# Four modulation pieces back on VectorE, an earlier first expert choice, and a choice's index work over both halves at once

## The reference, cut to what matters

```python
for i in range(4):                                   # mixers: GLA, SGU, FOX attention, GLA
    mod = silu(c) @ w_mod[i] + b_mod[i]              # 1024 -> 3072: shift, scale, gate
    h = rms_norm(x, norm_pre_g[i]) * (1 + scale) + shift
    x = x + gate * rms_norm(mixer_i(h), norm_post_g[i])
x = x + hybrid_mixer(rms_norm(x))                    # conv, three dilated attentions
u = rms_norm(x)
q = (u @ w_query).reshape(T, 8, 2, 128)              # 8 heads, two half queries
top_s, top_i = top_k(q . sub_keys, 16)               # 16 of 128 in each half
best_s, pos = top_k(top_s[0][:, None] + top_s[1][None, :], 16)      # 16 of 256 pairs
idx = top_i[0][pos // 16] * 128 + top_i[1][pos % 16]
x = x + sum(softmax(best_s) * gelu(u . down[idx]) * up[idx])        # 128 rows a token
```

## Time and profile before

| | |
|---|---|
| median of 3 runs | 1745.24 us (1738.43 to 1745.35) |
| the profiled execution: own time, span | 1739.41 us, 1737.6 us |
| PE, PEld, DVE, ACT, POOL busy | 80%, 41%, 60%, 25%, 28% of the span |
| mean granted clock of TensorE | 0.909 of full |
| moved by DMA | 591.53 MB, 340 GB/s over the span |
| rows of experts gathered by GpSimd | 312.56 MB with the pieces, 45.4% of 16 engines |
| chain that ended last | DVE 8%, DMA 8%, issue 3%, PE 1% |

### The profile page before, as it was taken

One profiled execution on the slowest core, in us unless ns is written; L12 is line 12 of the kernel. 1 busy time (PEld: TensorE's weight loads), 2 busy tenths in 40 slices (PEclk: granted clock), 3 DMA queues, 4 the chain that ended last, 5 costly groups with the idle time before them and its releaser, 6 DMA issues. The chain is left out here.

```text
span 1737.6 us, 13867 instructions
## 1 busy us (share of the span) xinstructions
PE 1393.7 (80%) x4158; PEld 717.6 (41%) x4158; DVE 1047.5 (60%) x2197; ACT 433.1 (25%) x974; POOL 490.7 (28%) x498
## 2 busy tenths in 40 slices
PE   6998988978999999999777777699787647666665
PEld 6454435444444455444354343455333312222222
DVE  3645554553233222313797998788866778877876
ACT  1221413423423421102133232132002221111111
POOL 2101210210000000000445546355344545444441
PEclk9998998989999999999897888798888878898898
DMA  9978884978556776887999989999999999999995
GB/s 386 377 256 303 312 340 171 347 282 295 213 207 219 277 265 242 290 293 265 402 361 357 413 339 403 412 400 413 410 414 414 348 412 422 421 422 421 422 421 248
DMA packets 108941, 591.53 MB, mean 340 GB/s; under 512 B 12450, under 2 KB 12706, under 8 KB 60612
## 3 DMA queue, kind: packets, MB, share of 16 engines
q0 software_dynamic: 67776, 312.56, 45.4%
q1 hardware_dynamic: 41092, 278.10, 42.2%
HBM read 589.55 MB, written 1.05 MB: 340 GB/s over the span
## 5 line engine op out<-in xcount | busy, mean ns | idle before, releaser
L948 PE MATMUL bank<-ring,hT 128*128 128x512 f32 x1888 | 866.6, 615 | 39.6 <-DVE room L1920 12.1
L948 PEld LDWEIGHTS bank<-ring,hT 128*128 128x128 f32 x1888 | 366.5, 198 | 482.2 <-issue 449.8
L877 POOL DMA_INDIRECT room<-in_peer_down,idx x92 | 102.5, 1114 | 525.1 <-DVE idx L1781 401.8
L1798 DVE CUSTOM_DVE_ANT_0 room<-room 128x1024 f32<-128x1024 f32 x180 | 218.6, 1221 | 50.6 <-DMA room<-in_pair,idx 38.4
L1203 PE MATMUL bank<-room 128*128 128x512 f32 x284 | 150.9, 676 | 96.5 <-ACT room L1493 94.2
L1813 DVE SCALAR_TENSOR_TENSOR x<-room,pcoef,x 128x1024 f32<-128x1024 f32 x121 | 155.7, 1287 | 28.0 <-DMA room<-in_peer_up,idx 27.5
L877 POOL DMA_INDIRECT room<-in_peer_up,idx x104 | 114.0, 1096 | 88.6 <-DVE pa L1798 42.3
L1203 PEld LDWEIGHTS bank<-room 128*128 128x128 f32 x284 | 57.5, 215 | 190.8 <-issue 97.2
L849 POOL DMA_DIRECT2D room<-in_w_mod x80 | 42.2, 528 | 326.3 <-DVE room L1567 206.5
L877 POOL DMA_INDIRECT room<-in_pair,idx x88 | 97.0, 1102 | 108.5 <-PE bank L1203 50.6
L927 PE MATMUL bank<-cst,room 128*128 128x128 f32 x424 | 64.7, 297 | 55.3 <-ACT room L1439 24.1
(11 more groups left out here) (304 smaller groups left out, 1527.4 us busy)
## 6 DMA issues: line engine op xcount, KB each, us to landing
ring<-in_wpk SPq DMA_DIRECT2D x248, 1024.0 KB, 7.0
room<-in_w_mod POOLq DMA_DIRECT2D x80, 512.0 KB, 8.2
room<-in_w_mod SPq DMA_DIRECT2D x8, 1024.0 KB, 15.8
room<-in_norm_post_g POOLq DMA_DIRECT2D x4, 512.0 KB, 5.0
rowb<-in_gate_bias SPq DMA_DIRECT2D x4, 512.0 KB, 9.0
room<-in_peer_up,idx POOLq DMA_INDIRECT x104, 12.5
room<-in_peer_down,idx POOLq DMA_INDIRECT x92, 12.4
room<-in_pair,idx POOLq DMA_INDIRECT x88, 14.3
```

Of the source, the lines that this page charges most:

```text
L877: return pool.indirect_dma_start(out=dst, out_offset=None, in_=A[table][0] if table != "pair" else A[table], in_offset=bass.IndirectOffset ...
L948: last = mm(bank[p][:, :], lhs, ring[:, h % 4, k * N:(k + 1) * N], start=(kk == 0), stop=(h == halves[-1] and k == 3))
L1798: v.tensor_tensor_reduce(out=row, in0=row, in1=u_(g // MINE), scale=1.0, scalar=0.0, op0=ALU.mult, op1=ALU.add, accum_out=pa[:, g // TOPK ...
```

## The change

It makes four kinds of edit.

1. Pieces 9, 11, 13 and 15 are summed on VectorE again; TensorE keeps 5 and 7.
2. A chunk's "mod" steps stand behind its "ev", the mixer's steps, "mod_cols" and "mod_gate", and ahead of what is pending; their numbers a block come from a table. One gap moves from behind layer 2's last output block to behind its fourth input block.
3. For tile 0, the first head's scores come one query block earlier, and so does its choice; the ticks stay where they are. In a choice three casts are left out, and the comparison, the product and the reduction work on both halves in one instruction each.
4. The last eight picks are added two a tick from tick 272 on, their last group of four is split in two, and picks 252 and 253 go to TensorE, 254 to VectorE.

```diff
 def out_chunks(t, L):
-            "gap twice"]
+            "gap" if L == 2 else "gap twice"]
...
             b(3, [], [("unit", t, 1), ("forget_sum", t)]),
+            "gap",
             b(4, [], [("quad_T", t, 0), ("quad_S", t, 0)]),
...
-            b(0, name="query", pre=[("norm_in", t, 5)]),
-            b(1, [("score_T", t, 0)], name="query"),
-            b(2, [("score_S", t, 0), ("score_T", t, 1)], name="query"),
+            b(0, [] if t else [("score_T", t, 0)], name="query", pre=[("norm_in", t, 5)]),
+            b(1, [("score_T", t, 0)] if t else [("score_S", t, 0)], name="query"),
+            b(2, ([("score_S", t, 0)] if t else []) + [("score_T", t, 1)], name="query"),
...
-TICKS = PICKS + REST + LEAD[1]
+TICKS = PICKS + REST + 2
-PE_PIECES = (5, 7, 9, 11, 13, 15)
+PE_PIECES = (5, 7)
...
 def on_vector(u):
-    return u < 7 * TOPK or u % 4 == 3 or (u % 2 and (u < MINE or u >= PICKS - 8))
+    return u < 7 * TOPK or (u % 4 == 3 and u < PICKS - 4) or (u % 2 and u < MINE) \
+        or u >= PICKS - 2 or (u % 2 and PICKS - 8 <= u < PICKS - 4)
...
 def added_at(v):
+    if v >= PICKS - 8:
+        return tick_of(PICKS - 2) + (v - PICKS + 8) // 2
     return tick_of(v) + LEAD[v // MINE]
...
-def pieces_at(mm):
-    if mm is None:
-        return 0
-    if mm[2] == "in0":
-        return (4, 4, 3, 2, 2, 2)[mm[3]]
-    return 4 + mm[3] if mm[2] == "out0" else 3
+PIECES_AT = {"in0": (4, 4, 4, 3, 3, 2), "out0": (4, 2), "in1": (4, 4, 4, 4, 3, 3), "out1": (3, 3),
+             "in2": (3, 3, 3, 3, 2, 2, 2, 2), "out2": (4, 2)}
...
         if mm:
             order.append(mm)
-        for _ in range(pieces_at(mm)):
-            if piece < len(PIECES):
-                order.append(("mod", piece))
-                piece += 1
         if mm and mm[2] in ("out0", "out1", "out2") and mm[3] == 1:
             order.append(("mod_cols", int(mm[2][3]) + 1))
...
+            for _ in range(PIECES_AT[name][n] if name in PIECES_AT else 0):
+                order.append(("mod", piece))
+                piece += 1
             order += pending
             pending = []
-            if name == "query" and n == 2:
+            if name == "query" and n == 1:
                 order.append(("choose", 0))
-                rows.tick()
-            if name == "query" and n == 3:
-                rows.tick()
-                rows.tick()
+            if name == "query" and n >= 2:
+                for _ in range(n - 1):
+                    rows.tick()
...
-                    v.tensor_copy(pixf[:, :, :], pix[:, :, :])
...
-                    link(v.tensor_copy(pabf[:, :, :], pab[:, :, :]))
                 elif part == 2:
-                    for c in range(2):
-                        last = v.tensor_tensor(hot[:, c, :, :], const("iota").unsqueeze(1).to_broadcast([P, TOPK, TOPK]),
-                                               pabf[:, c, :].unsqueeze(2).to_broadcast([P, TOPK, TOPK]), ALU.is_equal)
-                    link(last)
...
+                    both = [P, 2, TOPK, TOPK]
+                    link(v.tensor_tensor(hot, const("iota").unsqueeze(1).unsqueeze(1).to_broadcast(both),
+                                         pab[:, :, :].unsqueeze(3).to_broadcast(both), ALU.is_equal))
+                    link(v.tensor_tensor(hot, hot, pix[:, :, :].unsqueeze(2).to_broadcast(both), ALU.mult))
...
+                    link(v.tensor_reduce(psel[:, :, :], hot, X, ALU.add))
...
-                    v.tensor_copy(idx[:, w, :], pidf[:, :]).then_inc(S("picked"), 1)
+                    v.scalar_tensor_tensor(out=idx[:, w, :], in0=psel[:, 0, :], scalar=float(NK), in1=psel[:, 1, :],
+                                           op0=ALU.mult, op1=ALU.add).then_inc(S("picked"), 1)
```

More of the change, by code:

```diff
@@ L272 @@
 DVE_NTH = {u: i for i, u in enumerate(ON_DVE)}
-ADDS = {added_at(v): [v] for v in range(PICKS)}
+ADDS = {k: [v for v in range(PICKS) if added_at(v) == k] for k in range(TICKS)}
 def adds_of(k):
-    return ADDS.get(k, [])
+    return ADDS[k]
 def sums_at(hh):
@@ L289 @@
 EXP_AT = {sums_at(hh): hh for hh in range(T * PH) if hh != PH - 1}
-GROUPS = [(hh * TOPK, TOPK) for hh in range(PH)] + [(MINE + 4 * m, 4) for m in range(MINE // 4)]
+GROUPS = [(hh * TOPK, TOPK) for hh in range(PH)] + [(MINE + 4 * m, 4) for m in range(MINE // 4 - 1)] \
+    + [(PICKS - 4, 2), (PICKS - 2, 2)]
 GROUP_AT = {tick_of(g + n - 1) + 1: i for i, (g, n) in enumerate(GROUPS)}
 def group_of(v):
-    return v // TOPK if v < MINE else PH + (v - MINE) // 4
+    return next(i for i, (g, n) in enumerate(GROUPS) if g <= v < g + n)
 WAY = {"norm_in": 110, "low": 10, "decay": 12, "qk_T": 15, "level": 25, "cross": 30, "heads": 80, "gated_T": 50,
@@ L558, in build @@
         pix = sb("pix", [P, 2, TOPK], U32)
-        pixf = sb("pixf", [P, 2, TOPK])
         ppos = sb("ppos", [P, TOPK], U32)
         pab = sb("pab", [P, 2, TOPK], U32)
-        pabf = sb("pabf", [P, 2, TOPK])
         psel = sb("psel", [P, 2, TOPK])
-        pidf = sb("pidf", [P, TOPK])
         idx = sb("idx", [P, 4, TOPK], U32)
@@ L683, in build @@
         pk2, cand, cand2 = at(AA + 6144, 2 * P), at(AA + 6400, TOPK, TOPK), at(AA + 6656, TOPK * TOPK)
-        hot = at(AA + 6912, 2, TOPK, TOPK)
+        hot = at(AA + 6912, 2 * TOPK * TOPK).rearrange("p (c a b) -> p c a b", c=2, a=TOPK)
         diag = at(DIA, 4, P)
@@ L992, in _ @@
             pe.wait_ge(S("cond"), 1)
-            for piece in PE_PIECES[:2]:
+            for piece in PE_PIECES:
                 piece_columns(piece, use("mod_cols", 0)[1])
@@ L1002, in _ @@
                         pe.wait_ge(S(f"ev{p}"), n // 2)
-                    if L == 0:
-                        for piece in PE_PIECES[2:]:
-                            piece_columns(piece, p)
                     pe.wait_ge(S(f"sums_init{L % 2}"), sums_set(L))
@@ L1759, in choose @@
                     link(v.tensor_single_scalar(pab[:, 1, :], ppos[:, :], 15, ALU.bitwise_and))
-                    link(v.tensor_copy(pabf[:, :, :], pab[:, :, :]))
                 elif part == 2:
-                    for c in range(2):
-                        last = v.tensor_tensor(hot[:, c, :, :], const("iota").unsqueeze(1).to_broadcast([P, TOPK, TOPK]),
-                                               pabf[:, c, :].unsqueeze(2).to_broadcast([P, TOPK, TOPK]), ALU.is_equal)
-                    link(last)
[L1766 to L1769, removed]
-                else:
[L1771 to L1775, removed]
+                    both = [P, 2, TOPK, TOPK]
+                    link(v.tensor_tensor(hot, const("iota").unsqueeze(1).unsqueeze(1).to_broadcast(both),
+                                         pab[:, :, :].unsqueeze(3).to_broadcast(both), ALU.is_equal))
+                    link(v.tensor_tensor(hot, hot, pix[:, :, :].unsqueeze(2).to_broadcast(both), ALU.mult))
+                else:
+                    link(v.tensor_reduce(psel[:, :, :], hot, X, ALU.add))
                     if 4 <= hh < PH + 4:
```

## The result

The changed kernel takes 1756.44 us (median of 10 runs, 1751.95 to 1764.76), the kernel before 1744.86 (10 runs, 1738.43 to 1752.99): 1.0071 times as long, with a 95% interval of 1.0055 to 1.0087. It is slower, by 11.6 us at the medians. I had put 1741 as likeliest and 0.20 on slower by over 0.5%; the time is inside the range of 1720 to 1757 by half a us. Some 5 us of these are the scatter of single executions, as the profiled one of before was 5.5 us under its kernel's median and that of after is at its own. Two executions among all runs here, one of the kernel before and one of the version with the choice's instructions alone, took 2124 us at a granted clock of 0.64 and are in no ratio.

A forecast was written before the change was run, and what follows sets the result against it. TensorE's chain bounds the kernel until about 830 us, then mostly DMA. Terms 1.5 + 5.9 - 24 + 11.3 - 0.9 + 3.5 + 5 + 1.6 = 3.9 us less, predicting 1741 against the median; range 1720 to 1757.

The forecast's parts named there:

- Start and border to layer 1: Start: first block 9.0 us sooner, 1.5 kept (0 to 5). Layer 0 to 1: shorter piece wait, 5.9 gained (4 to 6).
- by 80 us: Sign against the prediction: TensorE's first levels come by 80 us; it expected the first level product at 83 to 85.
- Layer 1: SGU layer: twelve pieces ahead of the gate, 61 to 63 held up in GpSimd's queue; 24 us lost (15 to 28).
- Layer 2 and its output: Moved gap fills TensorE waits, 6.8; shorter piece wait, 2.8; layer 3's "mod_cols", 1.7; 11.3 us gained (6 to 15).
- nothing is lost: Layer 3's start: one block, 7 us, instead of two still covers the norm's about 6 us on VectorE and ScalarE.
- The first choice and the gathers: Transposes cost 0.9 us; six rows fetched sooner gain 3.5 (1.5 to 4); slots freed earlier gain 5 (0 to 9).
- three signs of being wrong: Pieces 61 to 63 landing within 3 us of issue; first levels by 80 us; DMA share 880 to 1060 us unchanged.
- The end: After the last dot product: fewer adds on TensorE, VectorE's last at +4.4 instead of +6.0; 1.6 us gained (1 to 2.5).
- The faster one: Rival, chance 0.34: pieces 61 to 63 land soon, SGU loss 12, start gives 4.5; near 1726 us (1716 to 1732).
- The slower one: Rival, chance 0.20: VectorE late at every gate, terms before 450 us at lower ends, 18 lost; near 1754 us.
- the choice's edits do nothing: Rival within the forecast: if the 5 us from shared stretches in the gathers are 0, the result is 1746 us.
- The Trainium skill's rule: Rival, 0.05 of the forecast's 0.46: pieces every 2.5 us, first gate some 3 us late instead of 6.5; near 1737.

The follow-up runs named there:

- new places alone: The changed kernel with layer 2's extra gap back behind its output blocks, all else as changed: 1745.01 us, 1.0020 of the kernel before.
- Later load alone: Choice, end and start edits on the kernel before, pieces and gap in old places, plus GpSimd's post-norm load eight pieces later: 1724.23 us, 0.9897.
- both together: The changed kernel with layer 2's gap back and GpSimd's post-norm load eight pieces later: 1734.20 us, 0.9947 of the kernel before.

## Why the prediction was wrong

**The sum.** I had 3.9 us gained; the profiled pair lost 16.7, a difference of 20.6 (11.6 lost at the medians, a difference of 15.5). Layer 2 makes 11.3 of the 20.6, start and border 6.6, the choice and the gathers 6.5 in this pair; layer 1 came out 3.9 better. By its terms:

- Start and border to layer 1, 1.5 and 5.9. Measured to A: 0.8. The border gained 4.7 for 5.9 (4.00 of the wait, 0.66 of the block): I had expected no fall of the clock behind a wait of 1 us and 2 us back for it, and the clock fell to 0.50 all the same. But of the 9 us of the start, which came as worked out (columns done at 36.95, first block at 38.77), nothing was left ahead of the border: TensorE stood 3.9 us behind. My chain had the last of pieces 24 to 27 done by 81 to 83; it ended at 85.2, and VectorE then made two levels (2.2 us) before TensorE could go on. The mechanism is the one I named, pieces fetched one by one as slots free, and its size was too small by 4 us. A "first level product" at 84.48 was also a wrong reading: level 0, which waits for no piece, stood at 80.93 and came at 74.21, so that "by 80 us" could not serve as a sign. Five kernels with the new places and the new start reach A at 173.1 to 173.8; four with the new start and the old places at 168.5 to 173.6, mean 171.7; five with the old of both at 170.0 to 178.0, mean 174.1. By these means start and border together are worth under 1 us, not 7.4.
- Layer 1, -24 (15 to 28). Measured -20.1, by the mechanism and at the places that I named. Sized too large by 4: the gate was 3.4 us later instead of 6.5, and piece 61 was added at 252.01, not near 255. Both pieces of the loss are shown: undoing the hold-up in GpSimd's queue returns 12.6 us of the stretch, and undoing the places returns all of it (169.4 us, before 172.1).
- **Layer 2 and its output, +11.3. This is the step that failed.** TensorE's lag was 19.3 us at B and 19.3 again at the block behind layer 3's norm (483.58, before 464.26): nothing gained. I had credited the moved gap with 6.8 and written of layer 3's start that "nothing is lost". The runs show the opposite: the pieces' new places alone make B to C 7 to 10 us shorter (451.4 us, against 458.5 to 461.2 in the four kernels that have the earlier choice but neither the new places in layer 2, nor the moved gap, nor the later load), and the gap takes 9.2 of these back (460.7). Later load alone, new places alone and both together give 450.4, 451.4 and 451.1: they use up the same slack, the late pieces. I had looked at what the moved block fills, and not at what it carries: its evacuation lands in ScalarE's queue behind the exponentials, and the block after it puts tile 1's centring in VectorE's queue ahead of tile 0's output.
- The first choice and the gathers, -0.9 + 3.5 + 5 = 7.6. The size is about right: with the end, these edits alone gave 10.5 us for my 9.2. The mechanism was not. I had the head start worth only the DMA time that it fills; it was kept whole, as the stretch of the gathers stayed as long as it was and started sooner. DMA's share between 880 and 1060 us is 0.94 before, 0.95 after, 0.95 with the choice's edits alone and 0.94 with the earlier place alone, so the holes there were hardly filled. The prediction named three signs of being wrong. This one, a share that stays as it was although VectorE is earlier, came true in those two. In the profiled pair B to C and the choice give 4.6 us and the gathers take 3.5, which is within their scatter of 900 to 910.
- The end, 1.6: measured 1.54 in the pair. The other four profiles with the old end show 8.77 to 9.46 us there, all nine with the new end 5.59 to 5.75, so that some 3 us is nearer the usual gain.

**The rivals.** The faster one (pieces 61 to 63 land soon) fell: VectorE had the first 8.0 us after its issue. The page of the kernel before would have told as much, since its median over all 80 pieces, from issue to landing, is 8.2 us:

```profile
room<-in_w_mod POOLq DMA_DIRECT2D x80, 512.0 KB, 8.2
```

The slower one had the right number, near 1754, from a different account: it wanted every early term at its lower end, with 18 lost before 450 us, and the lag there was 19.3. But layer 1's loss stood well inside its range and not at the end of it; two of the terms were at or below theirs for other reasons. Its premise, that VectorE is late at every gate, holds for the first levels and layer 1 and not for layer 2, where the new places gained. That the time lies inside my range, whose upper end came from this rival, is luck. The forecast's own lower end, 1733, was inconsistent: with 8.7 us as what can be told from no change, it should have been 1736.5. That the choice's edits do nothing fell too: with the end they are worth 0.6%.

The Trainium skill's rule that the queues of a DMA engine take turns (DMA: Bandwidth & Descriptors, "Queues, rings and completion order") would have given a piece every 2.5 us, an estimate. The rows after show 3.76 us from 229.01 to 232.77, as the rows before did, so the measurement stands. By the set-up of about 150 cycles, 0.16 us, that the Trainium skill gives for an instruction (VectorE: DVE Perf Modes, "Side-by-side: where the cycles go for N=2048 bf16"), a choice would have become 0.98 us shorter, an estimate. It became 0.71 shorter, for my 0.73 from the rows.

## What to carry to other kernels

Before moving a block of work into a wait, follow what it brings: which engine must empty its bank, what stands in that engine's queue ahead of it, and whose turn its next step takes. A wait filled on one engine can come back larger on two others. On a queue that only fetches, a load that waits for a late event belongs behind the fetches that don't. Here eight places further back were worth 9 us in the changed kernel; in the old order they took a wait of 6.07 us away in the trace, and the run times don't tell whether a gain is left. And where a stretch of transfers keeps its length whatever goes before it, as the gathers did here with DMA's share at 0.99 to 1.00 from 830 to 1700 us in all fourteen profiles, its start decides: count what reaches its first transfer, not the holes inside it. Why it keeps its length although DMA isn't full between 880 and 1060 us (0.92 to 0.95) is not shown.

## What the runs showed that I had not expected

Kernels with the same instructions up to A do not reach it at the same time: the five with the old start and the old places take 169.96, 173.12, 174.56, 175.07 and 178.01 us in their profiles. Terms of 1 to 5 us ahead of A can't be read from one pair of profiles. The cause is not shown.

Reading integers costs nothing that can be seen here: the product with `pix` as uint32 takes 692 ns for 512 elements, one of floats 686. By form, after:

```profile
L1756 DVE TENSOR_TENSOR room<-room,pix 128x512 f32<-128x512 f32 x16 | 11.1, 692 | 0.6
```
